# Output projection of the first eight heads as 16 jobs between the steps of the last attention

## The reference

```python
def c_mixer(u, uc, in_w, out_w, rpb, need_ctx):
    ...
    o = neighbourhood_latent(q, k, v, k_c, v_c, rpb)
    y = (o * jax.nn.silu(z)) @ out_w
...
    h = h + gate * y
return rms_norm_2(h, final_g)
```

## Time and profile before

| what | us |
|---|---|
| median of 3 runs (2910.15 to 2913.42) | 2911.48 |
| the profiled execution: its span | 2919.5 |
| PE busy in the span | 2735.7 |
| DVE, ACT, POOL busy | 1178.7, 651.8, 286.4 |
| from the end of na0 on PE to oc0's first product, idle | 1.00 |
| oc0, from its first product (2664.26) to pc1's first (2694.74) | 30.5 |
| na1, from its first score (2793.19) to oc1's first product (2878.70) | 85.5 |

### The profile page before, as it was taken

How to read it: one execution, slowest core, us unless ns; L and a number is a source line. 1 busy time by engine, 2 the same in 40 slices (tenths; PEclk the granted TensorE clock), 3 DMA queues, 4 the chain that set the end, 5 groups by cost and what they waited for, 6 DMA issues and landing times.

```text
span 2919.5 us, 35600 instructions
## 1 busy us (share of the span) xinstructions
PE 2735.7 (94%) x14398; PEld 1774.8 (61%) x14398; DVE 1178.7 (40%) x2628; ACT 651.8 (22%) x1372; POOL 286.4 (10%) x274
## 2 busy tenths in 40 slices
PE   8999999999999899999999989998799998999998
PEld 6858764554544576776753444443677667865864
DVE  5344443112122544424342111113654455665576
ACT  2130331123222200100020010000452452053053
POOL 2002001111110000000000111100200001112111
PEclk9999899999999999999999999999899999999999
DMA  5804348999999621232379999999200212220310
GB/s 184 324 1 147 116 169 348 418 413 416 378 416 368 260 87 58 87 116 90 127 299 401 421 420 419 413 417 409 85 30 32 67 39 84 75 81 30 98 26 37
DMA packets 118846, 613.33 MB, mean 210 GB/s; under 512 B 12813, under 2 KB 25165, under 8 KB 92944
## 3 DMA queue, kind: packets, MB, share of 16 engines
q1 hardware_dynamic: 96096, 546.17, 46.9%
q0 software_dynamic: 19904, 53.65, 5.4%
q10 hardware_dynamic: 2672, 11.09, 0.9%
HBM read 587.79 MB, written 38.80 MB: 215 GB/s over the span
## 4 chain that ended last, share of the span: by engine, by line
PE 74%; DMA 9%; DVE 7%; PEld 3%; ACT 3%; issue 2%; PEldq 0%; SPq 0%; ACTq 0%; DVEq 0%; POOLq 0%
PE psum L753 24%; PE psum L2324 11%; DMA ring<-in_expert_w_gu 8%; PE psum L889 6%; PE psum L2344 6%; PE psum L1015 5%; PE psum L653 5%; PE psum L1044 3%; PE psum L1033 3%; PE psum L643 3%; PE psum L1323 2%; PEld psum L753 2%; PE psum L2317 1%; DMA arena<-in_expert_w_gu 1%; DVE arena L1113 1%
## 5 line engine op out<-in xcount | busy, mean ns | idle before, releaser
L2324 PE MATMUL psum<-ring,XT 128*64 128x512 f32 x1024 | 245.4, 622 | 29.4 <-DMA ring<-in_expert_w_gu 28.3
L753 PE MATMUL psum<-arena 128*128 128x256 f32 x1056 | 239.1, 379 | 4.4 <-DVE arena L740 4.4
L2467 DVE TENSOR_TENSOR XT<-XT,psum 64x512 f32<-64x512 f32 x64 | 44.2, 690 | 489.4 <-ACT XT L2470 489.4
L2324 PE MATMUL psum<-arena,XT 128*64 128x512 f32 x1024 | 233.9, 601 | 6.1 <-DMA arena<-in_expert_w_gu 5.8
L753 PEld LDWEIGHTS psum<-arena 128*128 128x128 f32 x1056 | 200.0, 190 | 33.3 <-DVE arena L740 5.6
L1015 PE MATMUL psum<-arena 64*128 64x384 f32 (+7 forms) x736 | 191.7, 477 | 26.8 <-ACT arena L1069 15.9
L753 PE MATMUL psum<-XT,ring 128*128 128x256 f32 x864 | 196.7, 382 | 6.6 <-ACT XT L474 3.1
L753 PEld LDWEIGHTS psum<-XT,ring 128*128 128x128 f32 x864 | 164.5, 191 | 34.0 <-PEq L3448 6.1
L2324 PEld LDWEIGHTS psum<-ring,XT 128*64 128x64 f32 x1024 | 76.0, 142 | 175.9 <-issue 132.4
L889 PE MATMUL psum<-ring,arena 128*128 128x512 f32 x384 | 166.6, 593 | 4.4 <-DVEq L3448 2.0
L2324 PEld LDWEIGHTS psum<-arena,XT 128*64 128x64 f32 x1024 | 77.2, 138 | 140.3 <-issue 138.6
(11 more groups left out here) (399 smaller groups left out, 3941.4 us busy)
## 6 DMA issues: line engine op xcount, KB each, us to landing
ring<-in_expert_w_gu SPq DMA_DIRECT2D x64, 2048.0 KB, 18.4
arena<-in_expert_w_gu SPq DMA_DIRECT2D x64, 2048.0 KB, 20.4
arena<-in_expert_w_down SPq DMA_DIRECT2D x32, 2048.0 KB, 13.8
ring<-in_expert_w_down SPq DMA_DIRECT2D x32, 2048.0 KB, 12.0
ring<-in_ada_w SPq DMA_DIRECT2D x12, 2048.0 KB, 9.2
ring<-in_fox_w_in SPq DMA_DIRECT2D x8, 2048.0 KB, 12.7
ring<-in_ret_w_in SPq DMA_DIRECT2D x8, 2048.0 KB, 10.4
ring<-in_c_in_w SPq DMA_DIRECT2D x8, 2048.0 KB, 7.7
```

The source lines that it names most:

```text
L753: m = pe.matmul(ps[0][:, 2 * P * i:2 * P * (i + 1)], x, w, start=(not onto and i == 0 and c == 0), stop=(c == 3), skip_group_check=True)
L2324: i = pe.matmul(psum[side * BR:(side + 1) * BR, 0:FF], x[:, 4 * part + c, :], w[:, c, side * FF:(side + 1) * FF], start=(part == 0 and c = ...
```

## The change

`oc0` is no stage of its own any more. Its work is a list `a.inner` of `Products` in one bank (bank 7) that the attention `na1` carries along, so it comes after `pc1`. The list has 37 entries: one side job on DVE (the diagonals), four jobs that spread a quarter of the gate each (a fill of two products by PE, taken by ACT), and 16 pairs of a job (one token tile and a quarter of the columns: 4 products of 128x256 by PE, multiplied by the gate on DVE) and a side job on POOL (the sum into H). `share(n)` divides the list over the 38 steps: PE issues its share at the end of step n; ACT, DVE and POOL issue theirs of step n at the end of step n+1. The weighed results of `na1` use bank 6 alone (`OUT`), so that the first weighing of a pair waits for the multiply of the pair before. `ZT` of the first half moves from the arena, where the second half would overwrite it, to HC, the rows of the context. POOL's bias loads and band additions are spread over the steps in the same order as before, the additions two steps after the loads. The unit of `oc0` is now loaded after those of `pc1`, just ahead of that of `oc1`. `oc1` itself is unchanged.

```diff
--- before.py
+++ after.py
@@ -949,6 +949,20 @@
             LAG = 3
             table = 0
             nsink = rt[:, 11, 0:8]
+            OUT = 6, 7
+            inner = None
+
+            def share(self, n):
+
+                k, m = len(self.inner.jobs), len(self.steps())
+                return k * max(n, 0) // m, k * (max(n, -1) + 1) // m
+
+            def sp(self, sp):
+                if self.inner:
+                    self.inner.sp(sp)
+
+            def out_at(self, pair):
+                return self.OUT[pair % len(self.OUT)] * BANK
 
             def __init__(self, tag, heads, nq, window, scores, keys, v, out, add=None, sink=False, masks_on_pe=False):
 
@@ -1022,6 +1036,8 @@
                         self.turn(pe, u)
                     if u >= 2 and u % 2 == 0 and u <= self.units:
                         self.weigh(pe, u // 2 - 1)
+                    if self.inner:
+                        self.inner.pe(pe, *self.share(n))
 
             def turn(self, pe, u):
                 pe.wait_ge(self.s("norm"), self.at("norm") + u + 1)
@@ -1037,11 +1053,12 @@
                 k, h, i = self.unit[2 * m]
                 keys, pair, v = self.keys(2 * m), self.pair_of(2 * m), self.parts[k][3]
                 pe.wait_ge(self.s("pt"), self.at("pt") + self.first[2 * m + 2])
-                if i == 0 and pair >= 2:
-                    pe.wait_ge(self.s("out"), self.at("out") + pair - 1)
+                if i == 0 and pair >= len(self.OUT):
+                    pe.wait_ge(self.s("out"), self.at("out") + pair + 1 - len(self.OUT))
+                at = self.out_at(pair) + i * P
                 for n, kt in enumerate(keys):
                     for hh in range(2):
-                        ins = pe.matmul(psum[hh * DH:(hh + 1) * DH, (6 + pair % 2) * BANK + i * P:(6 + pair % 2) * BANK + (i + 1) * P],
+                        ins = pe.matmul(psum[hh * DH:(hh + 1) * DH, at:at + P],
                                         v(h + hh, kt), self.PT[:, m % 2, hh, n, :], start=(n == 0), stop=(n == len(keys) - 1))
                 ins.then_inc(self.s("weighed"), 1)
 
@@ -1068,6 +1085,10 @@
                             act.activation(sm[:, 3, n:n + 1], sinkb[:, h:h + 1], ACT.Exp, bias=sm[:, 0, n:n + 1])
                         act.activation(self.P[:, n % 4, 0:hi - lo], self.s_at(n, lo, hi), ACT.Exp,
                                        bias=sm[:, 0, n:n + 1], accum_out=sm[:, 1, n:n + 1]).then_inc(self.s("exp"), 1)
+                    if self.inner and n:
+                        self.inner.drains(act, "a", *self.share(n - 1))
+                if self.inner:
+                    self.inner.drains(act, "a", self.share(n)[0])
 
             def before_exp(self, act, n):
                 pass
@@ -1100,7 +1121,12 @@
                         k, pair, at = self.pairs[p]
                         out, nq = self.parts[k][4](pair), self.parts[k][5]
                         dve.wait_ge(self.s("weighed"), self.at("weighed") + u // 2)
-                        dve.tensor_tensor(out, bank(6 + p % 2)[:, 0:nq * P], out, ALU.mult).then_inc(self.s("out"), 1)
+                        o = psum[:, self.out_at(p):self.out_at(p) + nq * P]
+                        dve.tensor_tensor(out, o, out, ALU.mult).then_inc(self.s("out"), 1)
+                    if self.inner and n:
+                        self.inner.drains(dve, "v", *self.share(n - 1))
+                if self.inner:
+                    self.inner.drains(dve, "v", self.share(n)[0])
 
             def normalise(self, dve, n):
                 lo, hi = self.window(n)
@@ -3353,11 +3379,18 @@
                 return dve.tensor_scalar(m, m, -1.0, None, ALU.mult)
 
             def pool(self, pool):
-                for pair in range(1, self.heads // 2 - 1):
-                    pool.wait_ge(self.s("max"), self.at("max") + 2 * NT * pair)
-                    for h in range(2 * pair + 2, 2 * pair + 4):
-                        self.load(pool, h)
-                    self.band(pool, range(2 * pair + 2, 2 * pair + 4))
+                for n in self.steps():
+                    pair = n // (2 * NT)
+                    if n % (2 * NT) == 0 and 1 <= pair < self.heads // 2 - 1:
+                        pool.wait_ge(self.s("max"), self.at("max") + 2 * NT * pair)
+                        for h in range(2 * pair + 2, 2 * pair + 4):
+                            self.load(pool, h)
+                    if n % (2 * NT) == 2 and 1 <= pair < self.heads // 2 - 1:
+                        self.band(pool, range(2 * pair + 2, 2 * pair + 4))
+                    if self.inner and n:
+                        self.inner.drains(pool, "p", *self.share(n - 1))
+                if self.inner:
+                    self.inner.drains(pool, "p", self.share(n)[0])
 
             def band(self, pool, heads):
                 for h in heads:
@@ -3381,7 +3414,8 @@
             sevens = Sevens([region(18432 + 1024 * a, 4, 256) for a in range(4)], region(0, 4, 256), region(1024, 4, 256))
             for g in range(2):
                 QT, KT = region(6144, 2, 4, SEQ), region(10240, 8, NTA // 2 * P)
-                V, ZT = region(13312, NTA, 512), region(16384, 4, SEQ)
+                V = region(13312, NTA, 512)
+                ZT = region(16384, 4, SEQ) if g else HC[:, :, :].rearrange("p (r a) n -> p r (a n)", r=1).rearrange("p r (c n) -> p (r c) n", c=4)
                 p = BandProducts(f"pc{g}")
                 p.pairs = [(KT[DH:P, hh::2, P:3 * P], context_k_c[hh * DH:(hh + 1) * DH, 4 * g:4 * (g + 1), :]) for hh in range(2)]
                 p.pairs.append((V[:, NT:NTA, :], context_v_c[:, :, 512 * g:512 * (g + 1)]))
@@ -3421,11 +3455,38 @@
                                lambda r, ZT=ZT: ZT[:, r, :])
                 a.h0 = 8 * g
                 p.neighbours = a
-                u = Weights.add((0, 4, D, io["c_out_w_2"][0][512 * g:512 * (g + 1), :]))
-                if g:
-                    LastProj(f"oc{g}", u, 4, ZT, NT, 1).unit = u
-                else:
-                    use_units(OutProj(f"oc{g}", u, 4, ZT, NT, 1), u)
+                if not g:
+                    first_gate = ZT
+                    continue
+                us = [Weights.add((0, 4, D, io["c_out_w_2"][0][512 * k:512 * (k + 1), :])) for k in range(2)]
+                a.OUT = 6,
+                GATE, DIAG, TMP = region(18432, D), region(19456, KC, P), region(20480, 4, 256)
+                x = a.inner = Products("oc0", width=1, on=(7,)).inline()
+
+                def diagonals(dve, ps):
+                    for c in range(KC):
+                        i = dve.tensor_scalar(DIAG[:, c, :], ident, modc[:, 1, 16 + c, 0:1], None, ALU.mult)
+                    return i
+                laid = x.side("v", diagonals)
+                gate = []
+                for quarter in range(4):
+                    def fill(pe, ps, quarter=quarter):
+                        for c in range(2):
+                            i = pe.matmul(ps[0][:, c * P:(c + 1) * P], ones, DIAG[:, quarter * 2 + c, :], start=(c == 0), stop=(c == 1),
+                                          skip_group_check=True)
+                        return i
+                    gate.append(x.job("a", fill, lambda act, ps, quarter=quarter: act.activation(GATE[:, 256 * quarter:256 * (quarter + 1)], ps[0][:, 0:256], ACT.Copy),
+                                      after=[laid]))
+                sums = []
+                for n in range(4 * NT):
+                    t, at = n // 4, slice(256 * (n % 4), 256 * (n % 4 + 1))
+                    made = x.job("v", mm_R(us[0], 0, 4, D, at.start, 256, first_gate, t),
+                                 lambda dve, ps, n=n, at=at: dve.tensor_tensor(TMP[:, n % 4, :], ps[0][:, 0:256], GATE[:, at], ALU.mult),
+                                 units=(us[0],), release=(1,) if n == 4 * NT - 1 else (), needs=[gate[n % 4], *sums[max(0, n - 4):max(0, n - 3)]])
+                    sums.append(x.side("p", lambda pool, ps, t=t, n=n, at=at: pool.tensor_tensor(H[:, t, at], TMP[:, n % 4, :], H[:, t, at], ALU.add),
+                                       needs=[made]))
+                use_units(x, us[0])
+                LastProj("oc1", us[1], 4, ZT, NT, 1).unit = us[1]
 
         parts = [lambda: Start("start"), fox, lambda: moe(0, free_in_fox), retention, lambda: moe(1, free_in_retention),
                  mixer_a, mixer_b,
```

## The result

The changed kernel is slower: 2925.38 us median of 7 runs (2920.14 to 2929.22) against 2911.65 us of 7 runs of the kernel before, a ratio of 1.0047 (95% interval 1.0037 to 1.0057), that is +13.7 us. The forecast was +8.1 us; the range held the time.

What follows compares the result with a forecast made beforehand. PE was taken to set the end in both stages: -30.5 (oc0 removed) + 14.7 (na1's start) + 23.2 (from step 7) + 0.7 (na1's end) = +8.1 us, 2919.5 us; range 2914.5 to 2927.0 us.

Steps and rivals of the forecast that it cites:

- the case of half clock throughout: Rival for na1's start: all gate steps run at half clock, 5.9 us each; total +14.7 us, 2926 us; chance 0.12.
- full clock throughout: Good end for na1's start: gate steps wholly at full clock, score of step 7 at 2821.9, sum +6.3 us.
- PE sets the end in both stages, and oc0's removal is worth 30.5 us: PE works 29.5 of 30.5 us in oc0 and 78.2 of 84.5 in na1; dissolving oc0 gives -30.5 us.
- Weight ring and ZT's move, taken at nothing: Loading oc0's weights behind pc1's in the three-slot ring, and copying ZT to HC, cost nothing.
- The settled part: na1 from the score of step 7: 92.0 us, 23.2 more than before; products cover 2.7 us of waits.
- The list's places by the integer division, and the fills held by ACT's order: na1's start: step n gets entry n-1; PE's fills wait for ACT's gate copy behind the exponential; 11.2 us waiting.
- One gate step at half clock: na1's start: one gate step at half clock, about 5.9 us, the rest full; score of step 7 14.7 us later.
- The Trainium skill's rule on depth-cycling: Brief TensorE pauses while cycling PSUM buffers can swing its clock; read as all four gate steps at 1.2 GHz.
- the stretch from 329 to 345 us: Earlier attention in the old profile: clock stayed at 0.50 with PE 95% busy; cited as agreeing with the skill.
- The end of na1: PE's wait for DVE's multiply, POOL's sum and drain before oc1: 1.45 to 1.95 us, 0.7 more than before.
- The last stage unchanged: oc1, from its first product to the end: no term in the sum, so 0 us of difference.
- The gates don't hold PE: Rival for na1's start: ACT takes gates before the step's exponential, only 3.5 us added; total -3.1 us; chance 0.13.

Runs made afterwards that it cites:

- the run with the holes filled: Changed kernel plus 11 useless 128x512 products in PE's idle times at na1's start; ratio 1.0033 against the kernel before, start 31.2 us.
- ACT's share first: Changed kernel, but ACT takes the inner list's share at the start of its step, ahead of copies and exponential; ratio 1.0010 against the kernel before.
- diagonals first: Changed kernel, but DVE lays the eight diagonals before the first maximum; ratio 1.0038 against the kernel before, 0.9994 together with ACT's share first.

## Why the prediction was right, and where it was short

The mechanism is as forecast, and the range held the time; the forecast itself was 5.6 us short. By the traces the shortfall is 5.9 us: 3.2 us in the start, 0.5 in the settled part, 0.5 in the wait before the last stage and 1.7 in the last stage. The measured total lies 1.0 us from the case of half clock throughout (+14.7 us), but not by that case's way: that had the start at +21.3 us and nothing at the last stage. So the total by itself doesn't speak for it. The range's lower end, +3.0 us, doesn't follow from the bounds given: full clock throughout (+6.3) and the good end of the last wait (0.4 less) make +5.9.

- *PE sets the end in both stages, and oc0's removal is worth 30.5 us:* right, 30.5 us.
- *Weight ring and ZT's move, taken at nothing:* right, 98.46 us against 98.45 from pc1's first product to na1's first score.
- *The settled part:* right within 0.5 us (23.7 against 23.2). It was said that DVE had room enough beside POOL's additions; once in the attention it hadn't, 0.6 us.
- *The list's places by the integer division, and the fills held by ACT's order:* right in mechanism, shown by moving ACT's share alone. One of the four waits wasn't there: in step 5 the weighing at low clock covered it.
- *One gate step at half clock:* this term was mis-sized, in how many steps it falls on; a gate step wholly at the low clock was given 5.9 us (5.6 in the times that were added up, 2804.0 to 2809.6), and the first one, from fill to fill, took 6.1. The clock was at 0.50 in the first gate step, 0.70 in the second and 0.68 in the third. The scores of steps 4 to 7 came 17.1, 22.5, 27.8 and 33.5 us after the first, where the forecast had 16.4, 20.7, 24.9 and 30.4. The start cost 17.9 us, not 14.7; the case of half clock throughout (+6.6 us over the forecast) went too far.
- *The Trainium skill's rule on depth-cycling ("TensorE: Matmul & The Clock Gate", "A second HAM failure mode: psum-queue depth-cycling"):* the trace agrees that the clock goes down and comes back within such a train of short waits, and the run with the holes filled shows that it costs over 2 us here; it did not stay low through all four steps. The section speaks of a clock that swings, so "all four gate steps at 1.2 GHz" asked more of it than it says. And the stretch from 329 to 345 us, said to agree, is of another kind: PE waits once there (`329.99 0.48 PE L1033 MATMUL psum<-cst,arena 128*128 128x128 f32 x1 [0.85 <-DVE arena L1113]`), then works without a break, and the clock is 0.50 all the time.
- *The end of na1:* 2.24 us where 1.45 to 1.95 was worked out. POOL's sum ends at 2881.98, and PE starts 0.98 us later: the wait for POOL's drain and the hand-over were taken as 0.3 to 0.8 us.
- *The last stage unchanged:* wrong in this execution, 1.7 us by the low clock at its start. No term stood for it. Why the clock falls there in three of the six kernels with that wait is open.
- *The gates don't hold PE (-3.1 us):* refuted for the kernel as changed, and some microseconds too good as a price for its repair: with ACT's share first alone the trace has +1.6 us, with the diagonals first as well +1.2 us, and without the longer wait and the low clock at the end -1.8 us.

## What to carry to other kernels

Work moved between the steps of another loop costs no more than its own time only if no engine stands in line for it: look at where in its step each engine takes the job, and at what the issuer waits for if there is one buffer. A job taken at the end of a step, behind that step's slowest operation, holds the issuer for the whole chain; taken at the step's start, it cost PE no wait here. And if there is a hole that every execution has (here 3.5 us before the first exponential), short jobs with their own buffers belong there.

## What the runs showed of the hardware that was not expected

- Adding 11 products of no use made the start of the attention shorter, 31.2 against 33.5 us, with the granted clock at 1.00 through the gate steps.
- After a wait of 2.2 us, PE ran the next eight records in 3.67 us in three kernels and in 5.37 us in three others; five of the six run the same program in the 92 us ahead.
- A DVE scaling of 0.62 us took 2.51 us beside two POOL additions that ran 4.43 us together.
- The time up to na0's last weighing differed by 8.05 us between two profiled executions, 7.8 us of it before na0, where the kernels are the same; spans alone would have given +6.0 us for a change of +14.0.
